# Attention with unpadded value tiles, the two heads of a pair in alternating partition halves of PSUM, and the odd pairs' turned probabilities copied by ScalarE

## The chip, the cores and the metric

The kernel runs as one program on one NeuronCore of a Trainium2 chip. The metric is the time of one execution on the device, in microseconds (us); lower is better. The kernel before takes 5799.48 us (median of 3 runs, 5799.12 to 5800.59).

## The reference

A two-layer decoder trunk over 4096 tokens of width 1024. Layer 0 has a pooling mixer, a mixture of experts and a gated embedding; then one shared K and V are computed. Layer 1 has the attention that this change touches, and again experts and a gated embedding. The part that matters:

```python
HEAD_DIM = 64; N_Q_HEADS = 16; N_KV_HEADS = 4; WINDOW = 128; BLOCK = 128; SEQ = 4096

def swa_sink_attention(hn, w_q, w_o, sinks, k, v, cos, sin):
    ...
    kb = banded_blocks(k, nb)      # the block of 128 keys before and the own block
    vb = banded_blocks(v, nb)
    s = jnp.einsum('bnqkgd,bnjkd->bnkgqj', q, kb).astype(jnp.float32)
    ...
    s = jnp.where(mask, s, -jnp.inf)
    m = jnp.maximum(jnp.max(s, axis=-1, keepdims=True), sink)
    e = jnp.exp(s - m)
    pr = (e / (jnp.sum(e, axis=-1, keepdims=True) + jnp.exp(sink - m))).astype(vb.dtype)
    o = jnp.einsum('bnkgqj,bnjkd->bnqkgd', pr, vb).reshape(B, S, N_Q_HEADS * HEAD_DIM)
    return o @ w_o
```

Every product is accurate to about float32. The kernel splits an operand into two bf16 parts, hi and lo, and forms three products (hi x hi, hi x lo, lo x hi), or multiplies float32 directly.

## The kernel before, in words

The program is a row of phases with a barrier between them; the attention is one of them (`attention_phase`, from L1405). It walks over 32 blocks of 128 queries, one *step* each. Every engine has its own queue of instructions, written out by hand in this order, and semaphores tie them together. Nothing is scheduled automatically: an engine whose next instruction waits holds up all behind it. Steps -1, 0, 1 and the last four are written out, and a loop runs the others in twos. In step s an engine works on block s (`cur`), and still on what is left of blocks s-1 (`prev`) and s-2 (`prev2`).

The 16 query heads are 8 pairs, c = 0 to 7. One pair goes through these stages, with the lines of the functions:

- `scores` (TensorE, L1734): four records of a float32 matmul, two for each block of keys, into `ps_s`, which holds two pairs.
- `top` (VectorE, L1621 and L1626): adds the mask, takes the row's maximum, and its negative `nmx`.
- `exps` (ScalarE, L1559): the exponential of both heads, with the sum.
- `over` (VectorE, L1631): one over the sum. `heads` (GpSimd, L1536): hi part of the probabilities. `rests` (VectorE, L1638): their lo part.
- `turn` (TensorE, L1744): eight 128x128 transposes in bf16 into `ps_p`, which holds two pairs. It waits until pair c-2 has been copied out.
- `turned` (VectorE, L1647): copies the 128x1024 transposed values of a pair to `prT`.
- `weigh` (TensorE, mm3 L108 to L110, writing `ps_o`): probabilities times values, once for pairs 0 to 3 (jj = 0) and once for pairs 4 to 7 (jj = 1). The value tile `v` of a head is 128 columns wide, with the head's 64 values in one half and zeros in the other. So both heads of a pair accumulate into the same 128 partitions, in 12 matmuls of 512 columns.
- `out_hi` (ScalarE, L1566) and `out_lo` (VectorE, L1652): the two parts of the result, for `project` (TensorE, L108 to L110, writing `ps_x`), 4 times 12 matmuls.

The order around the change, for TensorE, at the end of step s: transposes of the next q and k (L1781, L1783), `turn(6)`, `weigh(s, 0)`, `scores(s+1, 0)`, `turn(7)`, `scores(s+1, 1)`; then in step s+1 `scores(2)`, `weigh(s, 1)`, the transposes of the normalised row `hn` (L1796), `turn(0)`, `scores(3)`, the first `project`. `scores(s+1, 0)` waits for ScalarE's copy `qT` (L1597), and the first `project` for ScalarE's copy `hnT` (L1579), since both read the PSUM tile `ps_x` that is reused. `weigh(s, 1)` waits for the copies of pairs up to 7. ScalarE's order there is: `exps(7)`, the square `junk` of the residual row (L1593), `qT`, `exps(s+1, 0)`, `out_hi(s, 0)`, `exps(s+1, 1)`, then `hrow` (L1575), `exps(2)`, `hnT`.

Of the kernel before, what the change touches and what calls it, by code (L numbers as in the profile page):

```python
# [24 lines left out]
ALU = mybir.AluOpType  # L25
# [1379 lines left out]
def attention_phase(nc, A, C):  # L1405
# [8 lines left out]
    with ExitStack() as stack:  # L1414
# [15 lines left out]

        kT = [m.sb(f"kT{u}", [P, 2, 2, P]) for u in (0, 1)]

        vp = [m.sb(f"v{u}", [P, 2, NKV, P], BF16) for u in (0, 1)]

        W = 2 * P
        score = [m.sb(f"score{c}", [P, 2, W + 1]) for c in range(NP)]
# [18 lines left out]
        q_ld, kv_ld, h3_ld, h4_st, row_st = ([m.sem(f"{n}{u}") for u in (0, 1)] for n in ("q_ld", "kv_ld", "h3_ld", "h4_st", "row_st"))  # L1455
        turn_mm, qT_done, kT_done, vh_done, v_done = m.sems("turn_mm qT_done kT_done vh_done v_done")

        s_mm, top_open, mx_done, nmx_done, e_done, rden_done, ph_done, pl_done, pT_mm, pT_done = m.sems(
            "s_mm top_open mx_done nmx_done e_done rden_done ph_done pl_done pT_mm pT_done")

        pv_mm, oh_done, ol_done, wo_mm, h4_done = m.sems("pv_mm oh_done ol_done wo_mm h4_done")
        ss_done, ms_done, rs_done, hn_done, hi_done, lo_done, hnT_mm, hnT_done, log_mm, log_done = m.sems(
# [22 lines left out]
        def pairs(t, c):  # L1485

            return NP * t + c + 1

        @block.sync
        def _(sp):  # L1490
# [61 lines left out]
        @block.scalar  # L1552
        def _(act):
            def exps(t, c):
                act.wait_ge(nmx_done, pairs(t, c))
                wait(act, pl_done, pairs(t, c - ER))
                for k in (0, 1):
                    n = 2 * c + k
                    e = act.activation(ex[c % ER][:, k, :], score[c][:, k, :], ACT.Exp, bias=nmx[:, n:n + 1],  # L1559
                                       accum_out=esum[:, n:n + 1])  # L1560
                e.then_inc(e_done, 1)

            def out_hi(t, jj):
                act.wait_ge(pv_mm, 2 * t + jj + 1)
                wait(act, wo_mm, 2 * t)
                act.activation(oT[:, 0, HALF * jj:HALF * jj + HALF, :], ps_o[:, jj, :].rearrange("p (i n) -> p i n", i=HALF),  # L1566
                               ACT.Copy).then_inc(oh_done, 1)

            def step(s, u, load, nxt, cur, prev, prev2):
                v = 1 - u  # L1570
                for c in range(NP):
                    if c == 0 and prev2:
                        act.wait_ge(hn_done, s - 1)
                        wait(act, row_st[u], done(s - 4, u) if not isinstance(s, int) or s >= 4 else 0)
                        act.activation(hrow[u][:, 0:D], hn[:], ACT.Copy).then_inc(hi_done, 1)  # L1575
                    if c == 1 and prev2:
                        act.wait_ge(hnT_mm, s - 1)
                        wait(act, log_mm, s - 2)
                        act.activation(hnT[:], ps_x[:], ACT.Copy).then_inc(hnT_done, 1)  # L1579
                    if c == 1 and prev:  # L1580
                        out_hi(s - 1, 1)
                    if c == 1 and cur:
                        act.wait_ge(kv_ld[u], done(s, u))
                        wait(act, pv_mm, 2 * s)
                        act.wait_ge(fixed, 4)
                        vin = kv_in[u][:, KVW:2 * KVW].rearrange("p (j k e) -> p j k e", k=2, e=HEAD)
                        for k in (0, 1):
                            last = act.activation(vp[u][:, 0, k:NKV:2, k * HEAD:k * HEAD + HEAD], vin[:, :, k, :], ACT.Copy)
                        last.then_inc(vh_done, 1)
                    if c == 6 and prev:  # L1590
                        act.wait_ge(h4_done, 2 * s)
                        wait(act, ss_done, s - 1)
                        act.activation(junk[:], h4[v][:], ACT.Square, accum_out=ss[:]).then_inc(ss_done, 1)  # L1593
                    if c == 6 and nxt:
                        act.wait_ge(turn_mm, s + 2)
                        wait(act, s_mm, NP * (s + 1))
                        act.activation(qT[:], ps_x[:], ACT.Copy).then_inc(qT_done, 1)  # L1597
                    if c == 7 and cur:
                        out_hi(s, 0)
                    if c < NP - 2 and cur:  # L1600
                        exps(s, c + 2)
                    if c >= NP - 2 and nxt:
                        exps(s + 1, c + 2 - NP)

            steps(act, step)

        @block.vector
        def _(dve):
# [33 lines left out]
            def turned(t, c):  # L1642
                jj, i = divmod(c, HALF)
                dve.wait_ge(pT_mm, pairs(t, c))
                if i == 0:
                    wait(dve, pv_mm, 2 * (t - 1) + jj + 1)
                dve.tensor_copy(prT[jj][:, :, i, :], ps_p[:, c % 2, :, :]).then_inc(pT_done, 1)  # L1647

            def out_lo(t, jj):
                dve.wait_ge(oh_done, 2 * t + jj + 1)  # L1650
# [12 lines left out]
            def step(s, u, load, nxt, cur, prev, prev2):  # L1663
                v = 1 - u
                for c in range(NP):
                    if c > 0 and cur:
                        turned(s, c - 1)
                    if c == 1 and prev:
                        out_lo(s - 1, 1)
# [3 lines left out]
                        over(s, c + 1)  # L1673
                    if c == 2 and cur:
                        dve.wait_ge(vh_done, s + 1)
                        vin = kv_in[u][:, KVW:2 * KVW].rearrange("p (j k e) -> p j k e", k=2, e=HEAD)
                        for k in (0, 1):
                            at = (slice(k, NKV, 2), slice(k * HEAD, k * HEAD + HEAD))
                            last = dve.tensor_tensor(vp[u][:, 1, at[0], at[1]], vin[:, :, k, :], vp[u][:, 0, at[0], at[1]],
                                                     ALU.subtract)  # L1680
                        last.then_inc(v_done, 1)
                    if c in (4, 5) and prev:
                        residual(s - 1, v, c - 4)
                    if c == 6 and prev2:
# [16 lines left out]
                        top(s, c + 2)  # L1701
                    if c == 7 and nxt:
                        top(s + 1, 0)
                    if c == 7 and cur:
                        turned(s, 7)
                    if c == 7 and nxt:
                        top(s + 1, 1)
                        over(s + 1, 0)
# [15 lines left out]
        def _(pe):  # L1724
# [12 lines left out]

            def turn(t, c):
                pe.wait_ge(pl_done, pairs(t, c))
                wait(pe, pT_done, pairs(t, c - 2))  # L1740
                for part in (0, 1):
                    for k in (0, 1):
                        for b in (0, 1):
                            mm = pe.transpose(ps_p[:, c % 2, 4 * part + 2 * k + b, :], pr[c % 2][:, part, k, b * P:(b + 1) * P],  # L1744
                                              C.ident_bf[:])
                mm.then_inc(pT_mm, 1)

            def weigh(t, par, jj):

                pe.wait_ge(pT_done, pairs(t, HALF * jj + HALF - 1))  # L1750
                pe.wait_ge(v_done, t + 1)
                wait(pe, ol_done, 2 * (t - 1) + jj + 1)
                out = ps_o[:, jj, :].rearrange("p (i n) -> p i n", i=HALF)
                n = 0
                for k in (0, 1):
                    for b, val in ((0, vp[1 - par]), (1, vp[par])):
                        hi, lo = (prT[jj][:, 4 * part + 2 * k + b, :, :] for part in (0, 1))
                        v_hi, v_lo = (val[:, part, 2 * jj + k, :] for part in (0, 1))
                        mm = mm3(pe, out, v_hi, v_lo, hi, lo, n == 0, n == 3)
                        n += 1  # L1760
                mm.then_inc(pv_mm, 1)

            def project(n, jj):
# [128 lines left out]
```

## Time and profile before

| what | value |
|---|---|
| median of 3 runs | 5799.48 us |
| profiled execution, whole | 5796.81 us |
| its span | 5795.1 us |
| TensorE (PE) busy | 5114.1 us, 88% |
| VectorE (DVE) busy | 3405.0 us, 59% |
| ScalarE (ACT) busy | 1949.0 us, 34% |
| GpSimd (POOL) busy | 1563.9 us, 27% |

The span runs from the first to the last instruction. Busy shares are averages over phases with different limits; the attention's steady steps lie between about 2800 and 3850 us of the span, and a stretch inside it is read by itself. A busy TensorE counts overlapping matmuls whose ends are modelled: of matmuls that follow each other the distance from start to start tells more than the duration.

### The profile page before, as it was taken

The numbers are of one execution on the slowest core, as the hardware profiler recorded it, in microseconds if no ns is written. First come the engines' busy times: TensorE is split into PE (matmuls) and PEld (weight loads), VectorE is DVE, ScalarE is ACT, GpSimd is POOL, SyncE is SP. The second block draws the span as 40 slices with busy tenths as digits, with TensorE's granted clock in tenths as the row PEclk, the third lists the DMA queues.
The fourth block names the chain that finished last, engine by engine and source line by source line (L and its number), as shares of the span: only waits on it lengthen the run. The fifth ranks groups of instructions, "written<-read, shape, count | busy, mean of one in ns | idle before, by whom it ended". The sixth has DMA issues, their size and how long they took to land. (4 is left out here: it accounts for less than half of the span.)

```text
span 5795.1 us, 103754 instructions
## 1 busy us (share of the span) xinstructions
PE 5114.1 (88%) x36100; PEld 3349.1 (58%) x36165; DVE 3405.0 (59%) x6738; ACT 1949.0 (34%) x2873; POOL 1563.9 (27%) x1159
## 2 busy tenths in 40 slices
PE   7939999999939999997799999965999999996998
PEld 7827767766724444443465665634776777673444
DVE  5665545544545555554688888875555555444665
ACT  6713333333322121111344444423433333322232
POOL 1124443333401110110222222213434443321222
PEclk9969999999969999998899999987999999998999
DMA  6736666666542222222221121105666666544443
GB/s 230 250 146 242 246 228 240 250 227 224 211 130 98 96 98 99 103 95 72 67 76 69 67 76 70 67 36 218 250 250 229 240 232 245 206 156 147 143 139 114
DMA packets 343205, 924.30 MB, mean 159 GB/s; under 512 B 39761, under 2 KB 51025, under 8 KB 343121
## 3 DMA queue, kind: packets, MB, share of 16 engines
q1 hardware_dynamic: 297040, 755.43, 35.7%
q0 software_dynamic: 46080, 167.79, 8.7%
q8 instruction: 48, 0.79, 0.1%
q14 instruction: 37, 0.30, 0.0%
HBM read 695.58 MB, written 227.54 MB: 159 GB/s over the span
## 5 line engine op out<-in xcount | busy, mean ns | idle before, releaser
L727 POOL TENSOR_TENSOR ex_w_lo<-ex_raw,ex_w_hi 128x2048 bf16<-128x2048 f32 x192 | 779.2, 4087 | 1338.5 <-ACT ex_w_hi L766 1338.4
L766 ACT ACTIVATE ex_w_hi<-ex_raw 128x2048 bf16<-128x2048 f32 x384 | 707.2, 1900 | 643.9 <-PE ex_ps_y L110 327.8
L883 PE MATMUL ex_ps_gate<-ex_xT,ex_w_hi 128*128 128x0 bf16 x2048 | 560.0, 274 | 37.2 <-ACT ex_silu L777 33.7
L853 DVE COPY ex_y<-ex_ps_y 128x512 f32 x324 | 223.9, 691 | 613.3 <-PE ex_ps_y L110 613.3
L884 PE MATMUL ex_ps_gate<-ex_xT,ex_w_hi 128*128 128x0 bf16 x2048 | 559.8, 274 | 0.0
L883 PE MATMUL ex_ps_up<-ex_xT,ex_w_hi 128*128 128x0 bf16 x2048 | 558.0, 273 | 1.9 <-issue 1.9
L885 PE MATMUL ex_ps_gate<-ex_xT,ex_w_lo 128*128 128x0 bf16 x2048 | 559.7, 274 | 0.0
L884 PE MATMUL ex_ps_up<-ex_xT,ex_w_hi 128*128 128x0 bf16 x2048 | 558.0, 273 | 0.0
L885 PE MATMUL ex_ps_up<-ex_xT,ex_w_lo 128*128 128x0 bf16 x2048 | 558.0, 273 | 0.0
L108 PE MATMUL ex_ps_y<-ex_w_hi,ex_aT 128*128 128x512 bf16 x1296 | 492.4, 380 | 41.3 <-DVE ex_xT L829 41.3
L835 DVE TENSOR_TENSOR ex_aT<-ex_silu,ex_ps_up 128x384 bf16<-128x384 f32 x256 | 141.6, 553 | 613.0 <-PE ex_ps_up L885 398.6
L109 PE MATMUL ex_ps_y<-ex_w_lo,ex_aT 128*128 128x512 bf16 x1296 | 491.7, 379 | 0.0
L110 PE MATMUL ex_ps_y<-ex_w_hi,ex_aT 128*128 128x512 bf16 x1296 | 491.7, 379 | 0.0
L1536 POOL TENSOR_TENSOR att_pr<-att_ex,att_rden 128x512 bf16<-128x512 f32 x256 | 270.5, 1057 | 793.5 <-DVE att_rden L1631 793.5
L1559 ACT ACTIVATE att_ex<-att_score,att_nmx 128x257 f32<-128x257 f32 x512 | 256.6, 503 | 572.6 <-DVE att_nmx L1626 571.8
L727 DVE TENSOR_TENSOR ex_w_lo<-ex_raw,ex_w_hi 128x2048 bf16<-128x2048 f32 x192 | 440.8, 2296 | 1.7 <-ACT ex_w_hi L766 1.7
L777 ACT ACTIVATE ex_silu<-ex_ps_gate 128x384 f32<-128x384 f32 x256 | 124.6, 488 | 814.8 <-PE ex_ps_gate L885 814.3
L108 PE MATMUL cb_ps_b<-cb_wg,cb_xT 128*128 128x512 bf16 x1024 | 390.4, 381 | 3.3 <-DVE cb_xT L1283 3.3
L109 PE MATMUL cb_ps_b<-cb_wg,cb_xT 128*128 128x512 bf16 x1024 | 390.1, 381 | 0.0
L110 PE MATMUL cb_ps_b<-cb_wg,cb_xT 128*128 128x512 bf16 x1024 | 390.0, 381 | 0.0
L1734 PE MATMUL att_ps_s<-att_kT,att_qT 128*128 128x256 f32 x1024 | 273.0, 395 | 1.1 <-ACT att_qT L1597 1.1
L1193 ACT ACTIVATE cb_junk<-cb_h 128x1024 f32<-128x1024 f32 x64 | 67.6, 1057 | 575.9 <-DVE cb_h L1257 575.9
(326 smaller groups left out, 10769.5 us busy)
## 6 DMA issues: line engine op xcount, KB each, us to landing
ex_raw<-in_w_exp_gate SPq DMA_DIRECT2D x128, 1024.0 KB, 9.6
ex_raw<-in_w_exp_up SPq DMA_DIRECT2D x128, 1024.0 KB, 11.1
ex_raw<-in_w_exp_down SPq DMA_DIRECT2D x128, 1024.0 KB, 6.4
y_rows<-ex_y SPq DMA_DIRECT2D x162, 512.0 KB, 4.0
cb_hin<-h_mid SPq DMA_DIRECT2D x64, 512.0 KB, 4.3
mix_x<-in_x SPq DMA_DIRECT2D x32, 512.0 KB, 4.4
h_mid<-mix_h SPq DMA_DIRECT2D x32, 512.0 KB, 5.0
y_rows<-mix_zeros SPq DMA_DIRECT2D x32, 512.0 KB, 5.7
```

The lines of the kernel that those rows point to most:

```text
L108: pe.matmul(out, lhs_hi, rhs_hi, start=first, stop=False)
L109: pe.matmul(out, lhs_hi, rhs_lo, start=False, stop=False)
L110: return pe.matmul(out, lhs_lo, rhs_hi, start=False, stop=last)
L727: eng.tensor_tensor(w_lo[u][:, w], raw[:, c, :], w_hi[u][:, w], ALU.subtract).then_inc(lo_done, 1)
L766: act.activation(w_hi[u][:, c * WCHUNK:(c + 1) * WCHUNK], raw[:, c, :], ACT.Copy).then_inc(hi_done, 1)
L853: dve.tensor_copy(y[:, bass.ds(j, 1), 512 * n:512 * n + 512].rearrange("p o d -> p (o d)"), ps_y[n][:]).then_inc(y_done, 1)
L883: pe.matmul(out, hi, x_hi, start=j == 0, stop=False)
L884: pe.matmul(out, hi, x_lo, start=False, stop=False)
L885: mm = pe.matmul(out, lo, x_hi, start=False, stop=j == KD - 1)
L1536: pool.tensor_tensor(pr[c % 2][:, 0, :, :], ex[c % ER][:, :, 0:W], rden[:, 2 * c:2 * c + 2].unsqueeze(2).to_broadcast([P, 2, W]), ALU.mult ...
L1559: e = act.activation(ex[c % ER][:, k, :], score[c][:, k, :], ACT.Exp, bias=nmx[:, n:n + 1], accum_out=esum[:, n:n + 1])
L1734: mm = pe.matmul(ps_s[:, c % 2, :, b * P:(b + 1) * P], qT[:, c, :], keys[:, jj, :, :], start=True, stop=True)
```

## The change

- The value tile of a head has 64 columns and no zeros. In `weigh`, head k of a pair writes partitions 64k to 64k+63 of `ps_o`, and the order of the twelve matmuls alternates between the two halves. Their number stays 12, with 512 columns each; each has 64 columns of weights.
- The hi and lo parts of the values are written by one instruction each, 128x256, where there were two of 128x128.
- `turned` of pairs 1, 3, 5 and 7 moves from VectorE to ScalarE. Each of the two engines gets a semaphore of its own for it; `weigh` waits for both, and `turn(c)` for the one that copies pair c-2. On ScalarE the copies stand at the head of c = 2, 4 and 6, and the one of pair 7 behind `exps(s+1, 1)`.

```diff
--- before.py
+++ after.py
@@ -1430,7 +1430,7 @@
 
         kT = [m.sb(f"kT{u}", [P, 2, 2, P]) for u in (0, 1)]
 
-        vp = [m.sb(f"v{u}", [P, 2, NKV, P], BF16) for u in (0, 1)]
+        vp = [m.sb(f"v{u}", [P, 2, NKV, HEAD], BF16) for u in (0, 1)]
 
         W = 2 * P
         score = [m.sb(f"score{c}", [P, 2, W + 1]) for c in range(NP)]
@@ -1455,8 +1455,9 @@
         q_ld, kv_ld, h3_ld, h4_st, row_st = ([m.sem(f"{n}{u}") for u in (0, 1)] for n in ("q_ld", "kv_ld", "h3_ld", "h4_st", "row_st"))
         turn_mm, qT_done, kT_done, vh_done, v_done = m.sems("turn_mm qT_done kT_done vh_done v_done")
 
-        s_mm, top_open, mx_done, nmx_done, e_done, rden_done, ph_done, pl_done, pT_mm, pT_done = m.sems(
-            "s_mm top_open mx_done nmx_done e_done rden_done ph_done pl_done pT_mm pT_done")
+        s_mm, top_open, mx_done, nmx_done, e_done, rden_done, ph_done, pl_done, pT_mm, pT_dve, pT_act = m.sems(
+            "s_mm top_open mx_done nmx_done e_done rden_done ph_done pl_done pT_mm pT_dve pT_act")
+        pT_done = [pT_dve, pT_act]
 
         pv_mm, oh_done, ol_done, wo_mm, h4_done = m.sems("pv_mm oh_done ol_done wo_mm h4_done")
         ss_done, ms_done, rs_done, hn_done, hi_done, lo_done, hnT_mm, hnT_done, log_mm, log_done = m.sems(
@@ -1485,6 +1486,10 @@
         def pairs(t, c):
 
             return NP * t + c + 1
+
+        def turns(t, c):
+
+            return HALF * t + c // 2 + 1
 
         @block.sync
         def _(sp):
@@ -1560,6 +1565,12 @@
                                        accum_out=esum[:, n:n + 1])
                 e.then_inc(e_done, 1)
 
+            def turned(t, c):
+                jj, i = divmod(c, HALF)
+                act.wait_ge(pT_mm, pairs(t, c))
+                wait(act, pv_mm, 2 * (t - 1) + jj + 1)
+                act.activation(prT[jj][:, :, i, :], ps_p[:, c % 2, :, :], ACT.Copy).then_inc(pT_act, 1)
+
             def out_hi(t, jj):
                 act.wait_ge(pv_mm, 2 * t + jj + 1)
                 wait(act, wo_mm, 2 * t)
@@ -1569,6 +1580,8 @@
             def step(s, u, load, nxt, cur, prev, prev2):
                 v = 1 - u
                 for c in range(NP):
+                    if c in (2, 4, 6) and cur:
+                        turned(s, c - 1)
                     if c == 0 and prev2:
                         act.wait_ge(hn_done, s - 1)
                         wait(act, row_st[u], done(s - 4, u) if not isinstance(s, int) or s >= 4 else 0)
@@ -1583,10 +1596,8 @@
                         act.wait_ge(kv_ld[u], done(s, u))
                         wait(act, pv_mm, 2 * s)
                         act.wait_ge(fixed, 4)
-                        vin = kv_in[u][:, KVW:2 * KVW].rearrange("p (j k e) -> p j k e", k=2, e=HEAD)
-                        for k in (0, 1):
-                            last = act.activation(vp[u][:, 0, k:NKV:2, k * HEAD:k * HEAD + HEAD], vin[:, :, k, :], ACT.Copy)
-                        last.then_inc(vh_done, 1)
+                        vin = kv_in[u][:, KVW:2 * KVW].rearrange("p (j e) -> p j e", e=HEAD)
+                        act.activation(vp[u][:, 0, :, :], vin, ACT.Copy).then_inc(vh_done, 1)
                     if c == 6 and prev:
                         act.wait_ge(h4_done, 2 * s)
                         wait(act, ss_done, s - 1)
@@ -1601,6 +1612,8 @@
                         exps(s, c + 2)
                     if c >= NP - 2 and nxt:
                         exps(s + 1, c + 2 - NP)
+                    if c == 7 and cur:
+                        turned(s, 7)
 
             steps(act, step)
 
@@ -1644,7 +1657,7 @@
                 dve.wait_ge(pT_mm, pairs(t, c))
                 if i == 0:
                     wait(dve, pv_mm, 2 * (t - 1) + jj + 1)
-                dve.tensor_copy(prT[jj][:, :, i, :], ps_p[:, c % 2, :, :]).then_inc(pT_done, 1)
+                dve.tensor_copy(prT[jj][:, :, i, :], ps_p[:, c % 2, :, :]).then_inc(pT_dve, 1)
 
             def out_lo(t, jj):
                 dve.wait_ge(oh_done, 2 * t + jj + 1)
@@ -1663,7 +1676,7 @@
             def step(s, u, load, nxt, cur, prev, prev2):
                 v = 1 - u
                 for c in range(NP):
-                    if c > 0 and cur:
+                    if c % 2 == 1 and cur:
                         turned(s, c - 1)
                     if c == 1 and prev:
                         out_lo(s - 1, 1)
@@ -1673,12 +1686,8 @@
                         over(s, c + 1)
                     if c == 2 and cur:
                         dve.wait_ge(vh_done, s + 1)
-                        vin = kv_in[u][:, KVW:2 * KVW].rearrange("p (j k e) -> p j k e", k=2, e=HEAD)
-                        for k in (0, 1):
-                            at = (slice(k, NKV, 2), slice(k * HEAD, k * HEAD + HEAD))
-                            last = dve.tensor_tensor(vp[u][:, 1, at[0], at[1]], vin[:, :, k, :], vp[u][:, 0, at[0], at[1]],
-                                                     ALU.subtract)
-                        last.then_inc(v_done, 1)
+                        vin = kv_in[u][:, KVW:2 * KVW].rearrange("p (j e) -> p j e", e=HEAD)
+                        dve.tensor_tensor(vp[u][:, 1, :, :], vin, vp[u][:, 0, :, :], ALU.subtract).then_inc(v_done, 1)
                     if c in (4, 5) and prev:
                         residual(s - 1, v, c - 4)
                     if c == 6 and prev2:
@@ -1701,8 +1710,6 @@
                         top(s, c + 2)
                     if c == 7 and nxt:
                         top(s + 1, 0)
-                    if c == 7 and cur:
-                        turned(s, 7)
                     if c == 7 and nxt:
                         top(s + 1, 1)
                         over(s + 1, 0)
@@ -1737,7 +1744,7 @@
 
             def turn(t, c):
                 pe.wait_ge(pl_done, pairs(t, c))
-                wait(pe, pT_done, pairs(t, c - 2))
+                wait(pe, pT_done[c % 2], turns(t, c - 2))
                 for part in (0, 1):
                     for k in (0, 1):
                         for b in (0, 1):
@@ -1747,17 +1754,17 @@
 
             def weigh(t, par, jj):
 
-                pe.wait_ge(pT_done, pairs(t, HALF * jj + HALF - 1))
+                for turned_by in pT_done:
+                    pe.wait_ge(turned_by, turns(t, HALF * jj + HALF - 1))
                 pe.wait_ge(v_done, t + 1)
                 wait(pe, ol_done, 2 * (t - 1) + jj + 1)
-                out = ps_o[:, jj, :].rearrange("p (i n) -> p i n", i=HALF)
-                n = 0
-                for k in (0, 1):
-                    for b, val in ((0, vp[1 - par]), (1, vp[par])):
-                        hi, lo = (prT[jj][:, 4 * part + 2 * k + b, :, :] for part in (0, 1))
-                        v_hi, v_lo = (val[:, part, 2 * jj + k, :] for part in (0, 1))
-                        mm = mm3(pe, out, v_hi, v_lo, hi, lo, n == 0, n == 3)
-                        n += 1
+                products = [(b, val, v_part, p_part) for b, val in ((0, vp[1 - par]), (1, vp[par]))
+                            for v_part, p_part in ((0, 0), (0, 1), (1, 0))]
+                for n, (b, val, v_part, p_part) in enumerate(products):
+                    for k in (0, 1):
+                        out = ps_o[HEAD * k:HEAD * k + HEAD, jj, :].rearrange("p (i n) -> p i n", i=HALF)
+                        mm = pe.matmul(out, val[:, v_part, 2 * jj + k, :], prT[jj][:, 4 * p_part + 2 * k + b, :, :],
+                                       start=n == 0, stop=n == len(products) - 1)
                 mm.then_inc(pv_mm, 1)
 
             def project(n, jj):
```

What this does to the order of ScalarE's queue is seen at the end of a step. The rows of the kernel before, from the exponentials of pairs 3 to 7 to the copy `hrow` of the next step:

```order
L1559 ACTIVATE att_ex,att_esum<-att_score,att_nmx 128x257 x10
L1593 ACTIVATE att_junk,att_ss<-att_h_1 128x1024
L1597 ACTIVATE att_qT<-att_ps_x 128x1024
L1559 ACTIVATE att_ex,att_esum<-att_score,att_nmx 128x257 x2
L1566 ACTIVATE att_oT<-att_ps_o 128x512
L1559 ACTIVATE att_ex,att_esum<-att_score,att_nmx 128x257 x2
L1575 ACTIVATE att_hrow<-att_hn 128x1024
```

And ScalarE in the changed kernel at the same place, from the exponentials of pairs 4 and 5:

```order
L1564 ACTIVATE att_ex,att_esum<-att_score,att_nmx 128x257 x4
L1572 ACTIVATE att_prT<-att_ps_p 128x8x128
L1564 ACTIVATE att_ex,att_esum<-att_score,att_nmx 128x257 x4
L1572 ACTIVATE att_prT<-att_ps_p 128x8x128
L1604 ACTIVATE att_junk,att_ss<-att_h_1 128x1024
L1608 ACTIVATE att_qT<-att_ps_x 128x1024
L1564 ACTIVATE att_ex,att_esum<-att_score,att_nmx 128x257 x2
L1577 ACTIVATE att_oT<-att_ps_o 128x512
L1564 ACTIVATE att_ex,att_esum<-att_score,att_nmx 128x257 x2
L1572 ACTIVATE att_prT<-att_ps_p 128x8x128
L1588 ACTIVATE att_hrow<-att_hn 128x1024
```

The copies `att_prT` are new in this queue: pair 5's stands between the exponentials and `junk`, and pair 7's behind the exponentials of the next block's pair 1.

TensorE around `weigh(s, 1)`, the last rows of it in the kernel before and what follows:

```order
L109 MATMUL att_ps_o<-att_prT,att_v 128x512
L110 MATMUL att_ps_o<-att_prT,att_v 128x512
L108 MATMUL att_ps_o<-att_prT,att_v 128x512
L109 MATMUL att_ps_o<-att_prT,att_v 128x512
L110 MATMUL att_ps_o<-att_prT,att_v 128x512
L1796 MATMUL att_ps_x<-all_ident,att_hn 128x128 x8
L1744 MATMUL att_ps_p<-all_ident_bf,att_pr 128x128 x8
```

TensorE in the changed kernel, from `scores(s+1, 1)` on:

```order
L1741 MATMUL att_ps_s<-att_kT,att_qT 128x2x128 x2
L1478 REGISTER_ALU
L1478 COMPARE_AND_BRANCH
L1741 MATMUL att_ps_s<-att_kT,att_qT 128x2x128 x2
L1766 MATMUL att_ps_o<-att_prT,att_v 64x512 x12
L1803 MATMUL att_ps_x<-all_ident,att_hn 128x128 x8
L1751 MATMUL att_ps_p<-all_ident_bf,att_pr 128x128 x8
```

The order of TensorE's groups is the same; the twelve matmuls of `weigh` now write 64 partitions each.

## Rows read from the trace of the kernel before

**Rows 1.** Stretch, us, busy PE PEld DVE ACT POOL (instructions), PEclk, DMA share, GB/s:

```profile
3200.00:3400.00 200.00, 184.17 (x1216) 119.82 (x1215) 163.26 (x506) 84.16 (x246) 54.00 (x54) 1.00 0.19 71
```

**Rows 2.** Waits in the attention: engine line <- releaser: us in total, times, longest:

```profile
ACT att_ex L1559 <- DVE att_nmx L1626: 571.8, 225, 4.8
PE att_ps_x L108 <- ACT att_hnT L1579: 52.9, 31, 1.7
```

**Rows 3.** TensorE in order of time, one step: start us, us, what:

```profile
3201.61 0.62 PE L1744 MATMUL att_ps_p<-all_ident_bf,att_pr 128*128 128x128 bf16 x8 [0.48 <-DVE att_pr L1638]
3202.07 0.38 PE L108 MATMUL att_ps_o<-att_prT,att_v 128*128 128x512 bf16 x1
...
3204.66 1.03 PE L1734 MATMUL att_ps_s<-att_kT,att_qT 128*128 128x256 f32 x4
3205.52 0.61 PE L1744 MATMUL att_ps_p<-all_ident_bf,att_pr 128*128 128x128 bf16 x8
3205.97 2.03 PE L1734 MATMUL att_ps_s<-att_kT,att_qT 128*128 128x256 f32 x8
3207.83 0.38 PE L108 MATMUL att_ps_o<-att_prT,att_v 128*128 128x512 bf16 x1
...
3211.01 1.09 PE L1796 MATMUL att_ps_x<-all_ident,att_hn 128*128 128x128 f32 x8 [0.42 <-DVE att_hn L1718]
3211.94 0.61 PE L1744 MATMUL att_ps_p<-all_ident_bf,att_pr 128*128 128x128 bf16 x8
...
3215.20 0.39 PE L108 MATMUL att_ps_x<-att_wo,att_oT 128*128 128x512 bf16 x1 [1.74 <-ACT att_hnT L1579]
...
3234.93 0.62 PE L1744 MATMUL att_ps_p<-all_ident_bf,att_pr 128*128 128x128 bf16 x8 [0.48 <-DVE att_pr L1638]
```

**Rows 4.** VectorE in order of time, same step:

```profile
3206.92 0.68 DVE L1647 COPY att_prT<-att_ps_p 128x1024 bf16<-128x1024 bf16 x1
3207.52 0.47 DVE L1621 CUSTOM_DVE_ANT_0 att_score<-att_ps_s,all_mask,att_sink 128x256 f32<-128x256 f32 x1
...
3208.73 0.69 DVE L1652 TENSOR_TENSOR att_oT<-att_ps_o,att_oT 128x512 bf16<-128x512 f32 x1
```

**Rows 5.** ScalarE in order of time, same step and the end of the next:

```profile
3207.12 0.51 ACT L1559 ACTIVATE att_ex<-att_score,att_nmx 128x257 f32<-128x257 f32 x1 [3.90 <-DVE att_nmx L1626]
...
3208.12 0.57 ACT L1566 ACTIVATE att_oT<-att_ps_o 128x512 bf16<-128x512 f32 x1
3208.72 0.51 ACT L1559 ACTIVATE att_ex<-att_score,att_nmx 128x257 f32<-128x257 f32 x1
...
3214.07 1.00 ACT L1579 ACTIVATE att_hnT<-att_ps_x 128x1024 f32<-128x1024 f32 x1
3214.97 0.58 ACT L1566 ACTIVATE att_oT<-att_ps_o 128x512 bf16<-128x512 f32 x1
...
3233.50 0.51 ACT L1559 ACTIVATE att_ex<-att_score,att_nmx 128x257 f32<-128x257 f32 x1 [2.86 <-DVE att_nmx L1626]
...
3234.50 1.04 ACT L1593 ACTIVATE att_junk<-att_h 128x1024 f32<-128x1024 f32 x1
...
3235.54 1.00 ACT L1597 ACTIVATE att_qT<-att_ps_x 128x1024 f32<-128x1024 f32 x1
```

**Rows 6.** TensorE after its two longest waits, in the first and last steps:

```profile
2788.44 1.03 PE L1744 MATMUL att_ps_p<-all_ident_bf,att_pr 128*128 128x128 bf16 x8 [2.58 <-DVE att_pr L1638]
...
3858.05 1.09 PE L1796 MATMUL att_ps_x<-all_ident,att_hn 128*128 128x128 f32 x8 [2.39 <-DVE att_hn L1718]
```

**Rows 7.** Busy time and clock around these waits:

```profile
2785.80:2788.00 2.20, 0.07 (x1) 0.00 (x0) 1.01 (x6) 1.30 (x6) 1.03 (x1) 1.00 0.00 0
2788.00:2791.40 3.40, 2.96 (x15) 2.30 (x16) 3.04 (x11) 1.49 (x6) 1.29 (x2) 0.50 0.00 0
2791.40:2794.80 3.40, 2.15 (x21) 1.67 (x20) 3.28 (x14) 1.09 (x4) 1.47 (x2) 1.00 0.00 0
...
3859.50:3863.00 3.50, 2.74 (x13) 2.74 (x14) 0.85 (x1) 0.70 (x1) 0.00 (x0) 0.54 0.38 152
```

## The prediction, made before the changed kernel was run

> **What bounds the kernel now.** I read the busy times of a stretch first, then the list of waits, then the timeline of one step engine by engine, since only this tells which queue is late where.
>
> The stretch is a steady piece of the attention. In it TensorE is busy 184 of 200 us, VectorE 163, ScalarE 84, and the granted clock is 1.00 [rows 1]. So TensorE looks like the bound, with VectorE not far behind. The waits say what the missing 8% is: TensorE waits 31 times, once per step, for ScalarE's copy `hnT`, 52.9 us in all [rows 2]. ScalarE itself waits almost 572 us for VectorE's `nmx`; it is idle much of the time, but always for the next link of the same chain.
>
> In the timeline one step takes 3234.93 - 3201.61 = 33.32 us, from `turn(6)` to `turn(6)` [rows 3]. Call the start of the first `project` T = 3215.20. From there TensorE works without a gap to the transposes of q and k, and waits 0.48 us before `turn(6)`. Then come `weigh(s, 0)` at 3202.07, `scores(0)` at 3204.66, `turn(7)`, `scores(1)` and `scores(2)`, `weigh(s, 1)` at 3207.83, the `hn` transposes at 3211.01 and `turn(0)`. The last wait ends at 3215.20, and this is what sets the end of the step [rows 3]. Followed back, it is a chain outside TensorE. `scores(0)` goes to `exps(0)`, 2.46 us after it; then `out_hi` at 3208.12, `out_lo` at 3208.73, `hn`, `rests(0)`, `top(2)`, `exps(2)`, and `hnT` at 3214.07 [rows 3 to 5]. From `scores(0)` to T are 3215.20 - 3204.66 = 10.54 us. So the step is two parts: T to the next `scores(0)`, and these 10.54 us. I ask what the change does to each.
>
> **The twelve matmuls of `weigh`.** They take 3204.66 - 3202.07 = 2.59 us, a slot of 0.216 us each [rows 3]. Their number and columns stay. No row of before shows two matmuls in different column halves, so the cost has two ends. If a pair shares a slot, a `weigh` takes 6 x 0.216 = 1.30 us; if each has its own, 2.59. Below 1.30 would need fewer columns, above 2.59 weight loads that no longer hide. The nearest row gives 2.59. I still take 1.30: the two matmuls of a pair use different columns and write different partitions, and neither needs the other. I keep 2.59 as a rival.
>
> The Trainium skill weighs in here (TensorE: Matmul & The Clock Gate, on packing small matmuls with row and column tiling): matmuls in different column groups of the array run side by side. No run here shows that yet. By it a `weigh` is 1.30 us, by the nearest row 2.59, and the sums below are 5806 and 5839 us.
>
> **T to `scores(0)`.** Before, `scores(0)` comes at 3237.98 (3204.66 plus one step), right behind `weigh(s, 0)`, so TensorE is the last there. Now VectorE no longer copies pair 5 at that place. `rests(6)` is earlier and the wait of 0.48 us goes: `turn(6)` at 3234.45, `weigh(s, 0)` at 3234.91, ended at 3236.21, or at 3237.50 if nothing overlaps. But `scores(0)` also needs `qT`. ScalarE's queue from 3233.50 is `exps(7)` 1.00 us, then the new copy of pair 5, then `junk` 1.04, then `qT` 1.00 [rows 5]. A ScalarE copy of 128x1024 out of PSUM takes 1.00 us, with the next start after 0.90 (3214.07 to 3214.97, rows 5). That one reads f32 and this one bf16; the bounds are the 0.69 us of the same copy on VectorE [rows 4] and the 1.04 of `junk`, which move the result by under 0.3 us each way. With 0.13 us from `hnT`'s end to TensorE's start (3215.07 to 3215.20): 3233.50 + 1.00 + 0.90 + 1.04 + 1.00 + 0.13 = 3237.57. So `scores(0)` is 0.41 us earlier, whichever way `weigh` goes; ScalarE takes TensorE's place as the last one, and of the 1.77 us that TensorE could have gained 1.36 turn into a wait for `qT`.
>
> **`scores(0)` to T.** VectorE saves a copy of 0.60 us between `top(0)` and `top(1)` (3206.92 to 3207.52, rows 4). It buys nothing: `out_lo` waits for `out_hi`, which ScalarE runs behind `exps(0)` at 3208.12, and neither moves against `scores(0)`. From `out_lo` on nothing changed. These 10.54 us stay, if TensorE delivers the `hn` transposes and `scores(3)` in time.
>
> That is the new danger, because the copy of pair 7 is now at ScalarE behind `out_hi` and `exps(1)`. `exps(1)` starts at 3208.72 + 33.32 - 0.41 = 3241.63, the copy at 3242.63, and it ends at 3243.63. `weigh(s, 1)` waits for it and starts at 3243.76; before, in the same count, at 3241.15. TensorE is through with `scores(2)` at 3240.74, so it stands still for 3.0 us in each step, where it did not wait before. Queued behind are all the `hn` transposes, `turn(0)` and `scores(3)`. With 1.30 for `weigh`, 0.93 for the transposes, 0.44 for `turn(0)` and 0.93 for `scores(3)` (half of 3205.97 to 3207.83) [rows 3], TensorE is ready at 3247.36. T is then at 3215.20 + 33.32 - 0.41 = 3248.11. The delay fits, with 0.75 us to spare.
>
> **The clock.** What rows show: TensorE waited 2.58 us before 2788.44 and 2.39 us before 3858.05 [rows 6]. Behind the first the granted clock was 0.50 (1.2 GHz) for 3.4 us and then 1.00 (2.4 GHz) again; behind the second it fell too, to 0.54 in the mean of the stretch [rows 7]. The waits of 1.74 us, 31 of them, cost no clock: it is 1.00 in the steady stretch [rows 1, 2]. The new wait of 3.0 us is longer than both that cost it. I expect the clock to fall behind most of these waits, and take three in four, for two of two such waits are a small sample and it will not catch each; the bounds are none and all. A fall halves TensorE's speed for 3.4 us, 1.7 us of lost work, of which 0.75 are covered: 0.95 us. Three in four give 0.71.
>
> **Smaller edits.** Value copies: one instruction of the same total width for two, on both engines, where ScalarE waits for `nmx` behind them anyway [rows 2]; nothing, and without that cover under 0.2 us. VectorE's other three copies (pairs 1, 3, 5): VectorE waits for TensorE there, except in the first step, where TensorE waits for VectorE's `pr` [rows 6]. Four copies of 0.60 are 2.4 us there; I take 2, bounds 0 and 2.4. The copies of pairs 1 and 3 on ScalarE run beside `scores` and `top`, before `exps` has its input.
>
> **The sum.** 30 steps x (-0.41 + 0.71) = +9, less 2 = +7 us on the profiled 5796.81 us (span 5795.1 and 1.7 around it). The median is 2.7 us above that execution: 5799.5 + 7 = 5806 us.
>
> The Trainium skill has a rule against the change (TensorEngine Tiling (Array Packing), Key Properties): a change of the tiling mode drains TensorE. The transposes and `scores` on both sides of a `weigh` are full size, so there are four changes a step. A matmul's end lies 0.38 - 0.22 = 0.16 us behind its slot [rows 3]. Three of four fall into waits; one a step would show when the clock is low, 30 x 0.16 = 5 us more, and the sum would be 5811. No run here shows it yet.
>
> **The rivals.**
> Clock holds. Then T is 0.41 us earlier per step: 30 x -0.41 - 2 = -14 us, 5785. For it speaks that both waits that cost the clock lay in first and last steps with thin work around them; against it that the new wait is longer.
> No overlap (the slower side). `weigh(s, 1)` ends at 3246.35, the `hn` transposes 1.09 us later at 3247.44, `hnT` starts at 3247.50 and T is 1.13 us behind it (3214.07 to 3215.20), 3248.63: 0.11 later than before. No slack is left, so a low clock costs its full 1.7 us. 30 x (0.11 + 0.75 x 1.7) - 2 = +40 us, 5839. It decides as soon as `weigh` takes over 1.30 + 0.75 = 2.05 us. The nearest row speaks for it. If the clock falls in every step it is 30 x 1.81 - 2 = +52, 5852.
> The copies hurt nothing and `weigh` sets the pace: both `weigh` calls faster, 30 x 2.6 = -78 us, 5722. Against it stand the 10.54 us that run outside TensorE and ScalarE's queue; for it nothing but TensorE's share of 92%.
>
> **How the numbers follow.** This kernel can tell 0.2% (12 us) from nothing. Forecast 0.50 (of it 0.02 faster, 0.38 same, 0.10 slower, by the share of steps that lose the clock: all would be 30 x 0.54 - 2 = +14). Clock holds 0.17 (0.11 faster, 0.06 same). No overlap 0.25 (0.23 slower, 0.02 same). `weigh` sets the pace 0.03, faster. Something unforeseen in ScalarE's order 0.05, slower. Together 0.16 faster, 0.46 same, 0.38 slower. The range reaches from the held clock, 5785, to the middle of the no-overlap case, 5842. The forecast's own is 5794 to 5814.
>
> **What would show it.** In the profile after: the distance of the first rows of `weigh` (0.22 us for two means overlap); a wait of about 3 us of TensorE before `weigh(s, 1)` put down to ScalarE's `prT`; a wait before `scores(0)` put down to `qT`, 1.4 us; a clock of about 0.95 in the steady stretch, against 1.00; the `hnT` copy still the last before `project`. The prediction is wrong if the wait before `weigh(s, 1)` is under 2 us, if the clock stays, or if `weigh` takes over 2 us.

## The result and the profile after

The changed kernel takes 5814.54 us (median of 9 runs, 5810.82 to 5817.35) against 5800.59 us before (9 runs). The ratio is 1.0022, with a 95% interval of 1.0012 to 1.0033: 14 us or 0.2% slower. The forecast was 5806, with its own range 5794 to 5814 and a whole range of 5785 to 5842; the measured time lies 0.5 us above the first and inside the second.

The profiled execution took 5814.91 us, its span 5813.2. Two stretches of the attention, with the columns of [rows 1]:

```profile
3000.00:3200.00 200.00, 176.64 (x1191) 117.42 (x1190) 148.57 (x466) 104.01 (x259) 52.03 (x53) 0.95 0.19 71
3200.00:3400.00 200.00, 176.30 (x1203) 115.00 (x1202) 149.36 (x468) 105.83 (x264) 53.30 (x54) 0.96 0.19 70
```

TensorE and VectorE are both less busy than before, by 8 and 14 us of 200, and ScalarE more. That looks like a gain, and the kernel is slower. The column before the last two has the reason: the clock is 0.95 to 0.96, not 1.00. The waits (columns of [rows 2]):

```profile
PE att_ps_o L1766 <- issue: 85.0, 31, 2.8
PE att_ps_s L1741 <- ACT att_qT L1608: 31.4, 31, 1.2
ACT att_hnT L1592 <- PE att_ps_x L1803: 26.5, 29, 1.2
```

TensorE now waits 31 times before `weigh(s, 1)`, 2.7 us each, and 31 times for `qT`. For the first the profile names no engine ("issue"); the timeline of ScalarE below shows which one was late. The last row is new: ScalarE's `hnT` waits for TensorE, where before TensorE waited for it. TensorE in one of the three steps of 31 in which the clock stayed up, start and us:

```profile
3210.65 1.49 PE L1766 MATMUL att_ps_o<-att_prT,att_v 128*64 128x512 bf16 x12
3213.13 1.13 PE L1741 MATMUL att_ps_s<-att_kT,att_qT 128*128 128x256 f32 x4 [0.99 <-ACT att_qT L1608]
...
3219.35 1.49 PE L1766 MATMUL att_ps_o<-att_prT,att_v 128*64 128x512 bf16 x12 [2.78 <-issue]
3220.77 1.09 PE L1803 MATMUL att_ps_x<-all_ident,att_hn 128*128 128x128 f32 x8
...
3223.54 0.39 PE L108 MATMUL att_ps_x<-att_wo,att_oT 128*128 128x512 bf16 x1 [0.31 <-ACT att_hnT L1592]
```

ScalarE of the kernel after in the same step:

```profile
3209.06 0.51 ACT L1564 ACTIVATE att_ex<-att_score,att_nmx 128x257 f32<-128x257 f32 x1 [3.75 <-DVE att_nmx L1639]
...
3210.06 1.00 ACT L1572 ACTIVATE att_prT<-att_ps_p 128x1024 bf16<-128x1024 bf16 x1
3210.96 1.04 ACT L1604 ACTIVATE att_junk<-att_h 128x1024 f32<-128x1024 f32 x1
...
3212.00 1.00 ACT L1608 ACTIVATE att_qT<-att_ps_x 128x1024 f32<-128x1024 f32 x1
...
3217.17 0.50 ACT L1564 ACTIVATE att_ex<-att_score,att_nmx 128x257 f32<-128x257 f32 x1
...
3218.16 1.00 ACT L1572 ACTIVATE att_prT<-att_ps_p 128x1024 bf16<-128x1024 bf16 x1
...
3222.41 1.00 ACT L1592 ACTIVATE att_hnT<-att_ps_x 128x1024 f32<-128x1024 f32 x1
```

The copy of pair 5 stands ahead of `junk` and `qT`, and `scores(0)` starts 0.13 us after `qT` ends. The copy of pair 7 ends at 3219.16, and `weigh(s, 1)` starts at 3219.35. A `weigh` is 1.42 us from its start to the next group (3219.35 to 3220.77), against 2.59 [rows 3]. And one step earlier, where the clock fell:

```profile
3185.45 1.71 PE L1766 MATMUL att_ps_o<-att_prT,att_v 128*64 128x512 bf16 x12 [2.80 <-issue]
3187.08 1.97 PE L1803 MATMUL att_ps_x<-all_ident,att_hn 128*128 128x128 f32 x8
3188.85 1.06 PE L1751 MATMUL att_ps_p<-all_ident_bf,att_pr 128*128 128x128 bf16 x8
...
3190.76 0.38 PE L108 MATMUL att_ps_x<-att_wo,att_oT 128*128 128x512 bf16 x1
```

Busy time and clock of two stretches behind that wait, same kernel:

```profile
3185.45:3186.55 1.10, 1.10 (x11) 0.61 (x12) 1.10 (x4) 1.05 (x1) 0.23 (x1) 1.00 0.00 0
3186.90:3190.20 3.30, 3.30 (x20) 3.03 (x19) 1.72 (x5) 2.13 (x6) 0.45 (x1) 0.53 0.21 88
```

The wait is as long as in the step above, and here it is followed by 1.1 us at full clock and then 3.3 us at 0.53: the `hn` transposes take 1.77 us to the next group, not 0.93. From the start of `weigh(s, 1)` to the first `project` are 5.31 us, against 4.19 in the step above. The fall costs 1.12 us in this step. In the whole trace it comes beside 28 of the 31 waits; the low stretch is 3.4 us long each time, and starts between 0.7 us before the start of `weigh(s, 1)` and 1.2 us behind it.

### The profile page after: what moved, and what is told of

Its sections match the earlier page's. It is cut to its first block and busy times, and to the rows that moved or that the text cites. A ratio compares the mean times of both kernels' runs of the same rounds, so it can differ in the third digit from the quotient of the medians.

```text
span 5813.2 us, 103873 instructions
## 1 busy us (share of the span) xinstructions
PE 5092.6 (88%) x36100; PEld 3342.9 (58%) x36165; DVE 3343.3 (58%) x6578; ACT 2065.6 (36%) x2969; POOL 1561.4 (27%) x1159
```

## The experiments

The theory: ScalarE's queue, not the narrow matmuls, cost the time, and it costs by the clock. The rivals: the narrow matmuls cost it, or the wait as such does. All times are medians. Each ratio is against runs of the kernel before that were made beside the experiment; their medians were 5801 to 5803 us. The diffs are shortened, and some comments in them are not in the kernels. Those of e5, e9 and e10 are against the columns alone, the others against the changed kernel.

**The columns alone** (e1_columns_only): `turned` stays on VectorE for all pairs.

```diff
-                    if c in (2, 4, 6) and cur:
-                        turned(s, c - 1)        # ScalarE; and pair 7 likewise
...
-                    if c % 2 == 1 and cur:
+                    if c > 0 and cur:
                         turned(s, c - 1)        # VectorE
```

> The unpadded values and alternating halves alone; all eight copies of a pair stay on VectorE. Queue theory (ScalarE's queue and the clock, not the narrow matmuls, cost the time): weigh takes about 1.4 us instead of 2.6, scores(0) comes 0.9 us earlier in each step because ScalarE has no copy of pair 5 ahead of qT, the clock holds at 1.00, and the kernel is 30 x 0.9 = 27 us faster than before, about 5773 us. Rival (the narrow matmuls and the changes of tiling mode cost what was lost): no faster than before, 5800 to 5815 us.

Measured: 5765.44 us, ratio 0.9940 (0.9926 to 0.9953). The columns alone win 36 us, 8 more than the theory said. The `hn` transposes, one step apart:

```profile
3198.69 1.09 PE L1793 MATMUL att_ps_x<-all_ident,att_hn 128*128 128x128 f32 x8 [1.59 <-DVE att_hn L1716]
...
3223.16 1.49 PE L1756 MATMUL att_ps_o<-att_prT,att_v 128*64 128x512 bf16 x12
3224.57 1.13 PE L1732 MATMUL att_ps_s<-att_kT,att_qT 128*128 128x256 f32 x4
...
3231.03 1.09 PE L1793 MATMUL att_ps_x<-all_ident,att_hn 128*128 128x128 f32 x8 [1.59 <-DVE att_hn L1716]
```

A step is 32.34 us, 0.98 less than before. Of the 2.3 us that the two `weigh` calls save, the one ahead of `scores(0)` pays; the other turns into a wait for `hn`, 1.59 us where it was 0.42 [rows 3].

**The copies alone** (e2_copies_only): the changed kernel with `v` padded to 128 columns and `weigh` in 12 full slots, as before.

```diff
-        vp = [m.sb(f"v{u}", [P, 2, NKV, HEAD], BF16) for u in (0, 1)]
+        vp = [m.sb(f"v{u}", [P, 2, NKV, P], BF16) for u in (0, 1)]
...
-                        out = ps_o[HEAD * k:HEAD * k + HEAD, jj, :].rearrange("p (i n) -> p i n", i=HALF)
-                        mm = pe.matmul(out, ...)
+                        mm = mm3(pe, out, v_hi, v_lo, hi, lo, n == 0, n == 3)
```

> ScalarE's copies of pairs 1, 3, 5 and 7 alone; values padded and weigh in 12 full slots as before. Queue theory: TensorE waits 3 us before weigh(s, 1), the clock falls in nine of ten steps, and weigh's full 2.6 us leave no slack: 30 x (0 + 0.9 x 1.7) = +46 us, about 5845 us. Rival (the copies are harmless, the narrow matmuls cost it): within 12 us of before or faster, 5785 to 5805 us.

Measured: 5837.43 us, ratio 1.0065 (1.0051 to 1.0079), the loss that the theory put on the copies. The size is 8 us off: in its trace the clock falls about every second step, not in nine of ten, and such a step is 34.8 us against 33.45. So the price of a fall with no slack was 1.4 us, not 1.7. ScalarE's `hnT` in three steps, a fall in the one between the first two:

```profile
3160.07 1.02 ACT L1592 ACTIVATE att_hnT<-att_ps_x 128x1024 f32<-128x1024 f32 x1 [0.51 <-PE att_ps_x L1810]
...
3194.89 1.02 ACT L1592 ACTIVATE att_hnT<-att_ps_x 128x1024 f32<-128x1024 f32 x1 [1.92 <-PE att_ps_x L1810]
...
3228.33 1.02 ACT L1592 ACTIVATE att_hnT<-att_ps_x 128x1024 f32<-128x1024 f32 x1 [0.52 <-PE att_ps_x L1810]
```

The wait before `weigh(s, 1)` is 2.8 us in each of these steps, and the clock falls beside 17 of 31 of them, where it is 28 of 31 in the changed kernel. So the length of a wait alone does not say whether the clock falls behind it.

**Pair 7's copy early** (e3_copy7_early): the changed kernel, one instruction moved.

```diff
+                    if c == 6 and cur:
+                        turned(s, 7)
                     if c >= NP - 2 and nxt:
                         exps(s + 1, c + 2 - NP)
-                    if c == 7 and cur:
-                        turned(s, 7)
```

> The changed kernel with the copy of pair 7 moved ahead of the exponentials of the next block's pair 0 on ScalarE, nothing else. Queue theory: the wait of 2.8 us before weigh(s, 1) goes, the longest wait in a step is about 2 us (for hn), the clock is 1.00 or nearly, and a step is 0.5 us shorter than before: 30 x -0.5 = -15, about 5785 us. Rival (the place in the queue does not matter, ScalarE's load does): 5810 to 5818 us as the changed kernel.

Measured: 5784.24 us, ratio 0.9970 (0.9959 to 0.9981), 30 us under the changed kernel. Its stretch from 3200 to 3400:

```profile
3200.00:3400.00 200.00, 172.16 (x1219) 114.47 (x1228) 152.89 (x479) 107.66 (x267) 54.72 (x56) 1.00 0.21 76
```

The clock is 1.00. The long wait is gone, but TensorE has not got less to wait for: 1.36 us for `hn` and 1.96 for `hnT` in each step stand in its place.

```profile
3208.28 1.09 PE L1803 MATMUL att_ps_x<-all_ident,att_hn 128*128 128x128 f32 x8 [1.36 <-DVE att_hn L1725]
...
3212.70 0.38 PE L109 MATMUL att_ps_x<-att_wo,att_oT 128*128 128x512 bf16 x1 [1.96 <-ACT att_hnT L1592]
```

Behind neither does the clock fall in the steady steps. So both the wait and the low clock went, and this run can't tell them apart.

**The wait filled** (e4_filled_wait): the wait for pair 7's copy stays, TensorE works in it.

```diff
+                if jj == 1:
+                    wait(pe, ol_done, 2 * (t - 1) + jj + 1)
+                    for _ in range(12):
+                        pe.matmul(ps_o[:, 1, :], C.ident_bf[:], wo[:, 0, 0, 0:512], start=True, stop=True)
                 for turned_by in pT_done:
```

> The changed kernel with twelve more matmuls of 512 columns on TensorE ahead of weigh(s, 1), where it waits for ScalarE; they write into the half of ps_o that weigh overwrites. They take 2.6 us of the wait of 3.0 and change nothing else. If the clock is what the wait costs: it stays at 1.00 and the time is about 5785 us, 30 us under the changed kernel, in spite of 372 matmuls more. If the wait itself or the queue behind it costs the time: 5814 us or more.

Measured: 5782.40 us, ratio 0.9970 (0.9957 to 0.9982). Twelve matmuls per block whose result is thrown away make the changed kernel 32 us faster. TensorE's busy time and the clock in the same stretch:

```profile
3200.00:3400.00 200.00, 189.35 (x1281) 122.74 (x1300) 153.62 (x485) 108.00 (x274) 54.72 (x55) 1.00 0.19 71
```

And ScalarE's `hnT` and `qT` of this kernel:

```profile
3207.41 1.00 ACT L1592 ACTIVATE att_hnT<-att_ps_x 128x1024 f32<-128x1024 f32 x1
3229.78 1.00 ACT L1608 ACTIVATE att_qT<-att_ps_x 128x1024 f32<-128x1024 f32 x1
```

The same two of the kernel with pair 7's copy early:

```profile
3211.34 1.00 ACT L1592 ACTIVATE att_hnT<-att_ps_x 128x1024 f32<-128x1024 f32 x1
3233.72 1.00 ACT L1608 ACTIVATE att_qT<-att_ps_x 128x1024 f32<-128x1024 f32 x1
```

They are 22.37 us apart in the one and 22.38 in the other. Both kernels have steady steps of 32.78 us, and so have the three steps of the changed kernel in which the clock stayed up, with the wait unfilled. So this wait costs nothing while the clock holds; the low clock behind it costs all 32 us.

**The halves one after the other** (e5_halves_in_turn): the columns alone, with the loop over k outside.

```diff
-                for n, (b, val, v_part, p_part) in enumerate(products):
-                    for k in (0, 1):
+                for k in (0, 1):
+                    for n, (b, val, v_part, p_part) in enumerate(products):
```

> The columns alone (all copies on VectorE), but weigh runs its six products of head 0 of each pair and then the six of head 1, so that neighbours use the same half of the array. If the gain of the columns is two neighbours side by side in different halves: weigh takes 12 slots of 0.216 us again, 2.6 us, a step is 33.6 us or a little more than before (the 0.26 and 0.12 us at the changes of width stay), about 5810 us. If narrow matmuls are quicker by themselves: 1.4 us and 5765 us as with the halves alternating.

Measured: 5784.04 us, ratio 0.9967 (0.9954 to 0.9981): between the two expectations, and both are wrong in size. A `weigh` takes 1.88 us, not 2.6:

```profile
3199.79 1.94 PE L1756 MATMUL att_ps_o<-att_prT,att_v 128*64 128x512 bf16 x12
3201.67 1.13 PE L1732 MATMUL att_ps_s<-att_kT,att_qT 128*128 128x256 f32 x4
```

Matmuls of this line that are under way, in slices of 0.05 us (busy and number of PE, then of the weight loads):

```profile
3199.95:3200.00 0.05, 0.05 (x1) 0.00 (x0) 1.00 1.06 246
...
3200.40:3200.45 0.05, 0.05 (x3) 0.00 (x0) 1.00 1.05 410
...
3200.80:3200.85 0.05, 0.05 (x4) 0.02 (x1) 1.00 1.23 492
...
3201.50:3201.55 0.05, 0.05 (x2) 0.00 (x0) 1.00 0.64 246
```

A recorded matmul lasts 0.38 us and the slots are 0.216, so one stream shows one or two at a time. Four at a time means two streams. The record does not name the half of a matmul, but its twelve starts are two rows of six with 0.22 to 0.24 us from start to start, one from 3199.79 and one from 3200.26. Read so, the second half starts 0.46 us after the first, when three of the first half's six, which stand ahead of it in program order, had not begun: TensorE ran the two halves side by side, out of program order.

**Five products less** (e10_seven): the columns alone, head 0 of each pair with its first product only.

```diff
                     for k in (0, 1):
+                        if k == 0 and n > 0:
+                            continue
```

> The columns alone (all copies on VectorE), but of the six products of head 0 of each pair only the first is made, so weigh has 7 matmuls and not 12; the output leaves those products out. If TensorE runs the two halves of the array side by side, the five that are gone cost nothing: weigh still takes 1.4 us, a step 32.34 us, 5765 us. If the halves only overlap in part, each one gone gives something back: up to 5 x 0.12 = 0.6 us a weigh, and with one of the two on the path 5747 us.

Measured: 5767.68 us, ratio 0.9938 (0.9922 to 0.9955), no faster than all twelve at 5765.44. `weigh` in its trace:

```profile
3225.59 1.49 PE L1758 MATMUL att_ps_o<-att_prT,att_v 128*64 128x512 bf16 x7
```

It is 1.49 us with 7 matmuls as with 12. With both halves in step, the five matmuls of the second are free.

**`qT` first** (e8_qt_first_late_ms): pair 7 early, and ScalarE in the order `qT`, `junk`, copy of pair 5; VectorE's `ms` moved from c = 6 to c = 7, behind `rests(7)`.

```diff
-                    if c in (2, 4, 6) and cur:
+                    if c in (2, 4) and cur:
...
+                    if c == 6 and cur:          # behind qT and junk
+                        turned(s, 5)
+                        turned(s, 7)
```

> The changed kernel with ScalarE in the order exps(7), qT, junk, copy of pair 5, copy of pair 7, exps(0), and VectorE's ms behind rests(7) so that it does not wait for junk. If qT behind the copy of pair 5 and junk is what ends T to scores(0): scores(0) moves to TensorE's own time, 1.3 us before that of the kernel before, a step is about 32.1 us, the clock is 1.00, and the time is 5801 - 30 x 1.2 = 5765 us. If ScalarE's order there does not matter once pair 7 is early: 5784 us.

Measured: 5755.43 us, ratio 0.9919 (0.9906 to 0.9933), 10 us under the expectation. Steps are 31.93 us:

```profile
3196.45 1.00 ACT L1592 ACTIVATE att_hnT<-att_ps_x 128x1024 f32<-128x1024 f32 x1
...
3228.38 1.00 ACT L1592 ACTIVATE att_hnT<-att_ps_x 128x1024 f32<-128x1024 f32 x1
```

Against pair 7's copy early, 0.85 us of a step were ScalarE's order around `qT`, with `ms` moved along with it; the two were not tried apart.

**Only pair 5's copy on ScalarE** (e9_copy5_only): the columns, and pair 5's copy behind `qT` and `junk`, the other seven on VectorE.

```diff
+                    if c == 6 and cur:          # ScalarE, behind qT and junk
+                        turned(s, 5)
...
-                    if c > 0 and cur:
+                    if c > 0 and c != 6 and cur:
                         turned(s, c - 1)        # VectorE
```

> The columns, with only the copy of pair 5 on ScalarE, behind qT and junk (qT first), VectorE's ms behind rests(7), and all other copies on VectorE. TensorE's wait of 0.48 us before turn(6) goes and qT is not late: a step is 31.9 us against 32.34 of the columns alone, 5765 - 30 x 0.45 = 5751 us. If VectorE's chain from top(0) to hn ends the step whatever comes before: 5765 us.

Measured: 5755.96 us, ratio 0.9918 (0.9905 to 0.9932), steps of 31.95 us. That is 5 us over the expectation. This and the one before are the best two, 47 us under the runs of before beside them and 59 under the changed kernel, and equal. Of four copies moved, one pays: `turn(6)` no longer waits its 0.48 us. It does not in the changed kernel either, where `ms` has its old place. What ends a step in both is the old chain: TensorE waits 1.46 us for `hn` and 1.96 for `hnT`:

```profile
3227.06 1.09 PE L1806 MATMUL att_ps_x<-all_ident,att_hn 128*128 128x128 f32 x8 [1.46 <-DVE att_hn L1724]
...
3231.48 0.38 PE L109 MATMUL att_ps_x<-att_wo,att_oT 128*128 128x512 bf16 x1 [1.96 <-ACT att_hnT L1589]
```

## Why the prediction was right

**`weigh`, 1.30 us.** Right. It is 1.42 us to the next group, and 12 matmuls last as long as 7. The rival without overlap (5839) describes the copies alone, and they took 5837. That they are so close is in part luck: the rival had 0.11 us and a fall in three of four steps at 1.7 us each, and that trace has 0.13 us and a fall in 17 of 31 steps, most at 1.4 us and two over 3.

**The change of width.** `weigh(s, 0)` starts 0.72 us after `turn(6)` (3209.93 to 3210.65), where it was 0.46 [rows 3], and ends 0.12 late. Of the first 0.26 us only a part is the width. Here is `turn(6)` in the kernel after and in the columns alone, and `turn(6)` and the first weight load of `weigh(s, 0)` in the copies alone:

```profile
3209.93 0.62 PE L1751 MATMUL att_ps_p<-all_ident_bf,att_pr 128*128 128x128 bf16 x8
```

```profile
3222.61 0.62 PE L1742 MATMUL att_ps_p<-all_ident_bf,att_pr 128*128 128x128 bf16 x8 [0.48 <-DVE att_pr L1640]
```

```profile
3215.22 0.62 PE L1757 MATMUL att_ps_p<-all_ident_bf,att_pr 128*128 128x128 bf16 x8
```

```profile
3215.93 0.10 PEld L108 LDWEIGHTS att_ps_o<-att_prT,att_v 128*128 128x128 bf16 x1 [0.27 <-issue]
```

With the columns alone it is 0.55 us (3222.61 to 3223.16), 0.09 over before. With the copies alone the full width stays, and it is 0.71 us. So 0.09 us is the way into the narrow matmuls and 0.12 the way out; I had 0.16 each. The other 0.17 us come with the copies. In all kernels that have them `turn(6)` does not wait, in the others it does; what delays `weigh` there stays open. The Trainium skill's rule in the prediction (TensorEngine Tiling (Array Packing), Key Properties: a change of the tiling mode drains TensorE) is in line with the 0.09 and 0.12 us; no run tells a drain from another cost of the change.

**T to `scores(0)`.** Right to 0.01 us: I had 22.37, and 22.37 is what the unthrottled steps show from `hnT` to the next `qT`, both with their 1.13 us behind. The copy of bf16 takes 1.00 us as assumed. The wait for `qT` is 0.99 us where I had 1.36, since TensorE comes to it 0.26 + 0.12 us later than I counted.

**`scores(0)` to T.** I had 10.54 us unchanged; it is 10.41 (3213.13 to 3223.54). The row of `hn` on VectorE is 1.38 us, where before has 1.61; `out_lo` ahead of it starts 0.10 us later behind `scores(0)` than before (4.17 against 4.07). Together that is the 0.13. So a step with full clock is 32.78, not 32.91. Why `hn` is shorter is told in the last section.

**The wait before `weigh(s, 1)`.** 3.0 forecast; 2.78 in the row, and 2.95 from slot to slot.

**The clock.** Right in kind; here are the two terms that were mis-sized. The share was 0.75 and is 0.9 in this kernel: a mean clock of 0.955 over 200 us is 9 us lost at half speed, or 5.3 stretches of 3.4 us in 5.9 steps. And the price was 0.95, with 1.12 in the step shown, because the slack was smaller: behind `weigh(s, 1)` the work ready at full clock takes 1.42 + 0.93 + 0.44 + 0.93 = 3.72 of 4.19 us, which leaves 0.47 us and not 0.75. In the step with the fall it is TensorE and no longer `hnT` that comes last before `project` (the row at 3190.76 has no wait). `hnT` gives the mean step, first and last of 29 rows:

```profile
2851.09 1.02 ACT L1592 ACTIVATE att_hnT<-att_ps_x 128x1024 f32<-128x1024 f32 x1 [0.51 <-PE att_ps_x L1803]
...
3797.74 1.02 ACT L1592 ACTIVATE att_hnT<-att_ps_x 128x1024 f32<-128x1024 f32 x1 [1.11 <-PE att_ps_x L1803]
```

It is 946.65 / 28 = 33.81 us, 0.49 over before; I had 0.30. 30 x 0.49 = 15 us, and this is the measured 14. With the measured terms: -0.54 + 0.9 x 1.12 = +0.47. The forecast had -0.41 + 0.71: the gain was 0.13 too small and the loss 0.3 too small, and that the two errors point against each other is luck.

**The first step, -2 us.** Not seen: from the first `scores` to the first of these `hnT` are 66.1 us before and 67.1 after (the first falls of the clock are in it). The forecast change of +7 us came out 7 us below the measured +14 by this and the clock together.

## What to carry to other kernels

- Ask of each wait that a change makes not only whether it has slack, but how long it is. A wait of 2.8 us that was covered in time still cost 32 us in all, because TensorE ran 3.4 us of the work around its end at 1.2 GHz in nine of ten steps; two waits of 1.4 and 2.0 us in its place cost no clock. Then look at the clock in the trace: beside the same wait it fell in 17 of 31 steps of the copies alone.
- In a hand-written queue the place of a moved instruction counts more than the engine's load. ScalarE was half idle, and a copy ahead of `qT` and one behind `exps(1)` took 0.85 and 1.0 us a step. Move the copy that is on the path, and put it behind what others wait for. (The 0.85 us include the new place of VectorE's `ms`.)
- When a change has two parts, time each alone: here -36 us and +36 us, with +14 for both. The two do not add up, so neither can be read from the sum.

## What the runs showed of the hardware

Two streams of narrow matmuls for different halves of the array run side by side here even where program order puts one behind the other: six and six in turn took 1.88 us, alternating 1.42, in full width 2.59. The start of the second stream was 0.46 us behind the first. How far ahead TensorE looks wasn't tried.

VectorE's `hn` gets longer beside GpSimd's `att_pr`. The two in the kernel after, GpSimd's first:

```profile
3217.18 1.03 POOL L1541 TENSOR_TENSOR att_pr<-att_ex,att_rden 128x512 bf16<-128x512 f32 x1 [4.19 <-DVE att_rden L1644]
```

```profile
3217.91 1.38 DVE L1725 SCALAR_TENSOR_TENSOR att_hn<-att_h,att_rs,att_g_ffn 128x1024 f32<-128x1024 f32 x1
```

And in the kernel before:

```profile
3208.84 1.03 POOL L1536 TENSOR_TENSOR att_pr<-att_ex,att_rden 128x512 bf16<-128x512 f32 x1 [5.36 <-DVE att_rden L1631]
```

```profile
3209.34 1.61 DVE L1718 SCALAR_TENSOR_TENSOR att_hn<-att_h,att_rs,att_g_ffn 128x1024 f32<-128x1024 f32 x1
```

`hn` starts 0.30 us before the end of GpSimd's row after, and 0.53 before: 0.23 us more beside it, and `hn` is 0.23 us longer. In a late block of the kernel before no GpSimd row lies beside it:

```profile
3839.13 1.28 DVE L1718 SCALAR_TENSOR_TENSOR att_hn<-att_h,att_rs,att_g_ffn 128x1024 f32<-128x1024 f32 x1
```

So `hn` is 1.28 us alone, 1.38 with 0.30 us of overlap and 1.61 with 0.53. In the steady steps of the other runs it is 1.61 where VectorE copies pair 7, and 1.38 or 1.42 where ScalarE does. The Trainium skill has this (SBUF — State Buffer, Who interferes with whom): VectorE and GpSimd share a pair of SBUF ports under an exclusive lock, and a VectorE instruction with two SBUF inputs contends with a GpSimd instruction that reads SBUF. These rows agree in that `hn` gets longer with the overlap; it wasn't tested by a run of its own.
